# A two-layer gated mixer block on one core: another order of the first products, tile transposes and small transfers

## The reference, cut to what matters

```python
for l in range(DEPTH):                                 # DEPTH = 2
    h = rmsnorm(x, norm_mix[l])
    x = x + hybrid_mixer(h, w_in[l], ...)              # splits h @ w_in into r_i, g_v, r_f, r_q, g_q, g_k, g_a, m_i, s_u, ...
    h = rmsnorm(x, norm_xattn[l])
    x = x + cross_attention(h, rmsnorm(mem, norm_mem[l]), xattn_w_q[l], xattn_w_kv[l], xattn_w_o[l])
    h = rmsnorm(x, norm_mlp[l])
    x = x + sq_relu_mlp(h, mlp_w1[l], mlp_w2[l])
return rmsnorm(x, norm_final)
```

## Time and profile before

| | us |
|---|---|
| median of 3 runs | 1950.54 |
| the three runs | 1950.54, 2742.40, 1949.77 |
| the profiled execution, device time | 1949.91 |
| its span | 1948.10 |
| TensorE busy in it | 1931.3 (99%) |
| VectorE, ScalarE, GpSimd busy | 1249.7, 961.8, 1127.9 |

### The profile page before, as it was taken

One profiled execution on the slowest core, in us unless ns is written; L12 is line 12 of the kernel. 1 busy time (PEld: TensorE's weight loads), 2 busy tenths in 40 slices (PEclk: granted clock), 3 DMA queues, 4 the chain that ended last, 5 costly groups with the idle time before them and its releaser, 6 DMA issues.

```text
span 1948.1 us, 33275 instructions
## 1 busy us (share of the span) xinstructions
PE 1931.3 (99%) x12707; PEld 1641.5 (84%) x12707; DVE 1249.7 (64%) x1909; ACT 961.8 (49%) x1665; POOL 1127.9 (58%) x1356
## 2 busy tenths in 40 slices
PE   7999999999999999999999999999999999999998
PEld 6788788888888889999887887888898888999997
DVE  5888778856145766767358786787641556667661
ACT  6754645345445644444456647353554655344334
POOL 4565564956834555766565555467576355566653
PEclk9999999999999999999999999999999999999999
DMA  6423233333422333333342233333343233333332
GB/s 187 119 73 85 82 83 88 87 109 107 148 82 81 99 99 102 99 103 98 98 102 79 72 87 82 81 83 87 120 130 124 66 98 95 111 104 98 103 98 81
DMA packets 196091, 191.41 MB, mean 98 GB/s; under 512 B 23834, under 2 KB 186204, under 8 KB 195548
## 3 DMA queue, kind: packets, MB, share of 16 engines
q1 hardware_dynamic: 194780, 187.19, 32.7%
q10 hardware_dynamic: 1152, 2.10, 0.3%
HBM read 185.04 MB, written 3.15 MB: 97 GB/s over the span
## 4 chain that ended last, share of the span: by engine, by line
PE 95%; ACT 2%; DVE 2%; DMA 1%; issue 0%; SPq 0%; POOL 0%; DVEq 0%; ACTq 0%
PE gemm L701 73%; PE mix L701 20%; DMA w_raw<-in_w_in_dram 1%; DVE work L1974 0%; DVE work L1965 0%; PE mix L1283 0%; DMA work<-in_norm_mix_dram 0%; DVE sums_raw L1965 0%; PE mix L944 0%; PE mix L1178 0%; ACT w_hi L1429 0%; ACT work L1819 0%; DMA w_raw<-in_mlp_w_dram 0%; PE mix L877 0%; ACT work_split L1579 0%
## 5 line engine op out<-in xcount | busy, mean ns | idle before, releaser
L694 POOL TENSOR_TENSOR w_lo<-w_raw,w_hi 128x256 fp32r<-128x256 f32 x676 | 584.8, 865 | 793.0 <-ACT w_hi L1429 793.0
L695 POOL TENSOR_TENSOR w_lo<-w_raw,w_hi 128x256 fp32r<-128x256 f32 x676 | 595.8, 881 | 0.0
L701 PE MATMUL gemm<-h_hi,w_hi 128*128 128x512 f32 x1248 | 493.7, 396 | 0.5 <-DVE h_lo L1974 0.5
L701 PE MATMUL gemm<-h_lo,w_hi 128*128 128x512 f32 x1248 | 486.2, 390 | 0.0
L701 PE MATMUL gemm<-h_hi,w_lo 128*128 128x512 f32 x1248 | 486.1, 390 | 0.0
L701 PE MATMUL gemm<-work_split,w_hi 128*128 128x512 f32 (+1 forms) x1552 | 446.9, 373 | 0.3
L1429 ACT ACTIVATE w_hi<-w_raw 128x512 fp32r<-128x512 f32 x676 | 380.0, 622 | 62.8 <-DMA w_raw<-in_w_in_dram 24.6
L701 PEld LDWEIGHTS gemm<-work_split,w_hi 128*128 128x128 f32 x1552 | 281.6, 189 | 51.0 <-DVE work_split L1974 1.1
L701 PE MATMUL gemm<-work_split,w_lo 128*128 128x512 f32 (+1 forms) x776 | 288.5, 372 | 0.0
L701 PEld LDWEIGHTS gemm<-h_hi,w_hi 128*128 128x128 f32 x1248 | 234.3, 188 | 56.7 <-issue 6.6
L701 PEld LDWEIGHTS gemm<-h_hi,w_lo 128*128 128x128 f32 x1248 | 234.3, 188 | 49.5
(11 more groups left out here) (372 smaller groups left out, 2792.9 us busy)
## 6 DMA issues: line engine op xcount, KB each, us to landing
w_raw<-in_mlp_w_dram SPq DMA_DIRECT2D x256, 256.0 KB, 2.7
w_raw<-in_w_in_dram SPq DMA_DIRECT2D x208, 256.0 KB, 2.7
w_raw<-in_xattn_w_kv_dram SPq DMA_DIRECT2D x64, 256.0 KB, 3.0
w_raw<-in_w_branch_dram SPq DMA_DIRECT2D x32, 256.0 KB, 2.7
w_raw<-in_w_out_dram SPq DMA_DIRECT2D x32, 256.0 KB, 2.7
w_raw<-in_xattn_w_q_dram SPq DMA_DIRECT2D x32, 256.0 KB, 2.8
w_raw<-in_xattn_w_o_dram SPq DMA_DIRECT2D x32, 256.0 KB, 2.7
w_raw<-in_w_in_dram SPq DMA_DIRECT2D x32, 128.0 KB, 3.5
```

The source lines that it names most:

```text
L694: pool.tensor_tensor(lo[:, 0:half], raw[:, 0:half], hi[:, 0:half].bitcast(F32), ALU.subtract)
L695: pool.tensor_tensor(lo[:, half:], raw[:, half:], hi[:, half:].bitcast(F32), ALU.subtract).then_inc(split_ready, 1)
L701: return pe.matmul(o, w, a, start=start, stop=stop, skip_group_check=True)
```

## The change

It has six parts.

1. **Products on zeros.** VectorE fills one 128x512 block of the scratch array `MG` with zeros, second of its instructions. TensorE multiplies these zeros before the first tile: twice 512 and once 256 columns, and once 512 more after the tiles are turned. The results are not used.
2. **Landing order.** Tiles are turned in the order 0, 1, 3, 2, and the gain just ahead of tile 3. The gain's load moves to ScalarE's queue, behind tiles 1 and 3.
3. **First weight unit on two queues.** Its `r_i` half comes from SyncE, its `g_v` half from ScalarE. The second halves of tiles 0 and 2 come after unit 1 in place of after unit 0.
4. **High by high first.** For layer 0, kc 0 and 1 on tiles 0 and 1, `opening` issues the high by high products of both tiles as soon as the high parts are there, then low by high, then high by low, with a wait ahead of each pair.
5. **Small transfers.** `s5_log_step` of both layers (four transfers) and the two narrow column loads are issued by ScalarE, between the high parts of units 7 and 8. The parameter rows of layer 0 come five at a time after units 8 to 11, the memory tokens after unit 11, those of layer 1 two at a time after units 15 to 24, the level masks after unit 25, and `w_a2`, `s5_b`, `s5_c` after unit 26 in place of 14. VectorE gets a wait for the masks.
6. **ScalarE's order.** `norm_hi` of layer 0 writes `h_hi` before it feeds the next unit, and `first` is 4 in place of 2, so that four columns stand ahead of `values_out("r_i")`.

The core of the diff:

```diff
-            sp.wait_ge(p_vec, 1)
-            sp.dma_start(Rf(24, 1)[0:KC, 0:P], norm_mix[0].rearrange("(a b) -> a b", b=P)).then_inc(p_x[0], 16)
@@ sync, unit 0
-                        for n in range(2):
+                        for n in range(2 if u else 1):
@@ sync, places of the small transfers
-                    if u == 0:
+                    if u == 1:
                         for t in (0, 2):
                             sp.dma_start(Rf(2 * t + 1, 1), x[0, t * P:(t + 1) * P, 512:]).then_inc(p_x2, 16)
                     if u == 8:
+                        sp.wait_ge(p_pe, 1)
+                        rows0, rows1 = param_rows(0, p_rows), param_rows(1, p_x[1])
+                    if 8 <= u < 12:
+                        for _ in range(5):
+                            next(rows0, None)
+                    if u == 11:
                         sp.dma_start(R(20, 4).rearrange("p (t a) b -> p t (a b)", t=2),
                                      mem[0].rearrange("(t p) d -> p t d", p=P)).then_inc(p_rows, 16)
-                        sp.wait_ge(p_pe, 1)
-                        for _ in param_rows(0, p_rows):
-                            pass
-                        rows1 = param_rows(1, p_x[1])
                         sp.wait_ge(p_pe, 7)
-                    if 13 <= u < 22:
-                        for _ in range(3):
+                    if 15 <= u < 25:
+                        for _ in range(2):
                             next(rows1, None)
+                    if u == 25:
+                        sp.dma_start(LM[:, :, :], level_masks.rearrange("p (l c) -> p l c", c=CH)).then_inc(p_dma, 16)
-                    if unit == (14 if L == 0 else 10):
+                    if unit == (26 if L == 0 else 10):
@@ tensor
+                def opening(kc, tiles):
+                    u, banks = u0 + kc, [(G[(s0, s1)[t // 2]][t % 2][:, :], slice(t * P, t * P + P)) for t in tiles]
+                    w_hi, w_lo = WHi[:, u % RING, :], WLo[:, u % RING, :]
+                    pe.wait_ge(u_hi, kc + 1)
+                    pe.wait_ge(split_hi, u + 1)
+                    for o, tok in banks:
+                        mm(o, Uhi[:, kc, tok], w_hi, start=kc == 0, stop=False)
+                    pe.wait_ge(u_ready, kc + 1)
+                    for o, tok in banks:
+                        mm(o, Ulo[:, kc, tok], w_hi, start=False, stop=False)
+                    pe.wait_ge(split_ready, u + 1)
+                    for o, tok in banks:
+                        mm(o, Uhi[:, kc, tok], w_lo, start=False, stop=False)
+            def keep_busy(n):
+                for _ in range(n):
+                    mm(G[1][1][:, :], MG[:, 7, 0:P], MG[:, 7, :])
+            pe.wait_ge(v_chain, 1)
+            keep_busy(2)
+            mm(G[1][1][:, 0:256], MG[:, 7, 0:P], MG[:, 7, 0:256])
+            for t in (0, 1, 3):
+                pe.wait_ge(p_x[t], (32, 16, 16, 32)[t])
+                if t == 3:
+                    pe.transpose(G[0][0][:, 0:P], Rf(24, 1)[:, 0:P], ident).then_inc(p_pe, 1)
+                x_columns(t, range(4), XB)
+            pe.wait_ge(p_x[2], 16)
+            for k in range(4):
+                x_columns(2, (k,), XB).then_inc(p_pe, 1)
+            keep_busy(1)
@@ scalar
+            act.wait_ge(p_vec, 1)
+            act.dma_start(Rf(24, 1)[0:KC, 0:P], norm_mix[0].rearrange("(a b) -> a b", b=P)).then_inc(p_x[3], 16)
+            act.dma_start(WR[:, 0, BW:], w_in[0][0:P, COL["g_v"]:COL["g_v"] + BW]).then_inc(raw_in[0], 16)
@@ scalar, start of layer 0
-                first = 6 if L else 2
+                if L == 0:
+                    feed(first_unit("r_i") + 8)
+                    for l, landed in ((0, p_rows), (1, p_x[1])):
+                        for a in range(2):
+                            src = s5_log_step[l].rearrange("(t a) -> a t", a=2)[a:a + 1, :]
+                            act.dma_start(SM[64 * a:64 * a + 64, 16 + 8 * l:24 + 8 * l],
+                                          src.to_broadcast([64, 8]), allow_slow_non_contiguous=True).then_inc(landed, 16)
+                    for what, wide, to in (("m_i", 8, 0), ("g_a", RANK, 8)):
+                        src = w_in[0][:, COL[what]:COL[what] + wide].rearrange("(k p) c -> p k c", p=P)
+                        act.dma_start(NW[:, :, to:to + wide], src, allow_slow_non_contiguous=True).then_inc(nw_in, 16)
+                    feed(first_unit("r_i") + 10)
+                first = 6 if L else 4
@@ vector
             do(dve.memset(R(24, 2)[:, :, 0:P], 0.0), p_vec)
+            do(dve.memset(MG[:, 7, :], 0.0))
+                if L == 0:
+                    dve.wait_ge(p_dma, 32)
                 pick(hg, 0)
```

More of the change, by code:

```diff
@@ L538, in _ @@
                 sp.dma_start(Rf(2 * t, 1), x[0, t * P:(t + 1) * P, 0:512]).then_inc(p_x[t], 16)
-            sp.wait_ge(p_vec, 1)
-            sp.dma_start(Rf(24, 1)[0:KC, 0:P], norm_mix[0].rearrange("(a b) -> a b", b=P)).then_inc(p_x[0], 16)
             def param_rows(l, landed):
                 stage = Rf(24 + l, 1)[:, 0:P]
-                for a in range(2):
-                    src = s5_log_step[l].rearrange("(t a) -> a t", a=2)[a:a + 1, :]
-                    sp.dma_start(SM[64 * a:64 * a + 64, 16 + 8 * l:24 + 8 * l],
-                                 src.to_broadcast([64, 8]), allow_slow_non_contiguous=True).then_inc(landed, 16)
-                    yield
                 for name, src in (("norm_mix", norm_mix), ("norm_xattn", norm_xattn), ("norm_mem", norm_mem),
@@ L629, in _ @@
                                      src.rearrange("(k p) c -> p k c", p=P)).then_inc(raw_in[u % RING], 16)
-                    if u == 12 or (L < DEPTH - 1 and (name, part) == ("up1_0", 0)):
-                        nl = L if u == 12 else L + 1
+                    if L < DEPTH - 1 and (name, part) == ("up1_0", 0):
+                        nl = L + 1
                         for what, wide, to in (("m_i", 8, 0), ("g_a", RANK, 8)):
@@ L778, in token_values @@
                         pe.wait_ge(gemm_free[s0][b], used0)
-                products(0, (0, 1))
-                products(1, (0, 1))
+                for kc in range(2):
+                    if now[0]:
+                        products(kc, (0, 1))
+                    else:
+                        opening(kc, (0, 1))
                 yield
@@ L947, in params @@
             def params(l):
-                pe.wait_ge(p_x[1] if l else p_rows, 16 * 22 if l else 16 * 23)
+                pe.wait_ge(p_x[1] if l else p_rows, 16 * 22)
                 pe.transpose(M[3 - l][:, 0:P], Rf(24 + l, 1)[:, 0:P], ident).then_inc(p_pe, 1)
@@ L962, in _ @@
             XB = lambda k: (M[0], M[1], M[2], M[3], M[0], M[1], M[2], M[3])[k]
-            pe.wait_ge(p_x[0], 48)
-            pe.transpose(G[0][0][:, 0:P], Rf(24, 1)[:, 0:P], ident).then_inc(p_pe, 1)
-            for t in range(TT):
-                if t:
-                    pe.wait_ge(p_x[t], 16)
-                if t < TT - 1:
-                    x_columns(t, range(4), XB)
-                else:
-                    for k in range(4):
-                        x_columns(t, (k,), XB).then_inc(p_pe, 1)
+            def keep_busy(n):
[13 more added lines that the diff above has]
+            keep_busy(1)
             for L in range(DEPTH):
@@ L1490, in norm_hi @@
                 for k in range(k0, k1):
-                    feed(first_unit("r_i") + 8 + k)
+                    if now[0]:
+                        feed(first_unit("r_i") + 8 + k)
                     act.wait_ge(*of_layer(hx_ready, k + 1))
                     do(act.activation(Hhi[:, k, :], TH[:, k % 2, :] if now[0] else M[1 + k % 2], ACT.Copy), hi_ready)
+                    feed(first_unit("r_i") + 8 + k)
             def values_out(name):
@@ L1599, in _ @@
                     t = k - 1
-                    act.wait_ge(p_x[t], 48 if t == 0 else 16)
+                    act.wait_ge(p_x[t], (32, 16, 16, 32)[t])
                     act.wait_ge(p_x2, 16 * TT)
@@ L1618, in _ @@
                 if L == 0:
-                    act.wait_ge(p_rows, 16 * 23)
+                    act.wait_ge(p_rows, 16 * 22)
                     for t in range(2):
```

1 line of the change is left out of this document (removed).

## The result

The changed kernel takes **1963.05 us** (median of 4 runs, 1961.15 to 1963.52), where the kernel before took 1950.22 beside it. The ratio is 1.0066, with a 95% interval from 1.005 to 1.0082: 12.8 us slower. The forecast of 1947.0 was wrong, and so was its range, which ended at 1952.5. The executions that were profiled differ by as much: 1962.78 after, 1949.91 before; spans 1961.0 and 1948.1. Nearly all of the 12.9 us can be found in the first 94 us.

What follows compares the result with a forecast made beforehand. TensorE, busy 1931.3 of 1948.1 us, was taken as the bound, leaving 16.8 us idle to win. 2.65 + 0.5 + 0.3 = 3.5 us off 1949.9 gave 1946.4, plus 0.6 for the median 1947.0; range 1945.5 to 1952.5.

Steps and rivals of the forecast that it cites:

- Products on zeros, tiles and gain: Opening: sixteen transposes 0.11 us apart, not 0.21, saving 1.6 us; column 0 stands at about 7.8, not 10.7.
- Unit 0: First weight unit: some 300 KB less moved ahead of it, 0.8 us, so landed at 8.2 instead of 8.98.
- First products: TensorE through the opening's products at 13.0 instead of 15.91, 2.9 us won.
- Does it stay ahead?: From the opening to `r_f`: slack covers VectorE's and ScalarE's smaller lead, so `r_f` could start at 34.85, 2.9 us early.
- rival C: The start is won but given back at a formerly covered wait, losing up to 2.9 us: about 1949.5; chance 0.10.
- the chain to 81 us: ScalarE and VectorE work ending in a parameter column; expected some 4 us earlier, removing TensorE's 0.3 us wait.
- The copy of the `r_i` results: Ahead of `r_f`: it starts 5.8 us after `h_hi` 0, at 31.1 + I; with I at 4.0, 35.1, 2.65 us early.
- I: Time ScalarE takes to issue the six small transfers from about 24 us; taken as 4.0 us.
- How long is I?: Step setting I at 4.0 us from single SyncE issues; one stall (8.9) and two (13.8) stay in the range.
- two bounds: For I: unhindered SyncE issues, 3.4 to 4.1 us together; or stalls in a full queue, 4.88 and 2.92 us seen.
- Rival A: The queue fills under ScalarE; win is 7.5 less I; one stall gives 1952.0, two 1956.9; chance 0.25.
- The other waits: TensorE's waits inside `r_f` (0.5 us, late weight unit) and at 81 us (0.3 us, parameter column) both go.

Runs made afterwards that it cites:

- e6: The changed kernel with steps in 64-byte runs (e4), without the products on zeros: 1946.65 us.
- e11: e4 with the gain behind tile 2 on SyncE and turned first, tiles in the order 0, 1, 2, 3: 1946.60 us.
- e7: e4 with the old product order for kc 0 and 1: 1946.97 us. Its text gives ScalarE's first high part in ten executions, 7.63 to 9.07 us.
- e10: e4 with unit 0 whole on SyncE and the second halves of tiles 0 and 2 right behind it, as before: 1947.76 us.
- e4: The changed kernel with each layer's steps sent as 64-byte runs to 128 rows, sorted by a VectorE copy, still on ScalarE: 1946.46 us.
- e1: The changed kernel with the two column loads back on SyncE, the step transfers staying on ScalarE: 1953.67 us.
- e2: The changed kernel with the four step transfers back on SyncE, the column loads staying on ScalarE: 1947.21 us.
- e3: The changed kernel with all six small transfers (steps and column loads) back on SyncE: 1947.30 us.
- e5: The kernel before with only the step transfers changed to 64-byte runs, on SyncE at the old place: 1949.08 us.
- e8: The changed kernel with only layer 0's pair of steps on ScalarE ahead of the column loads, layer 1's back on SyncE: 1951.61 us.
- e12: The changed kernel with 20 unused products keeping TensorE busy ahead of the transpose that waits before `r_f`: 1960.61 us.

## Why the prediction was wrong, point by point

- **Products on zeros, tiles and gain: right, but worth little.** Transposes stood 0.11 apart from 6.23 on. The 1.6 us they save lay almost wholly beside ScalarE's work and the landing of unit 0: e6 puts the zeros at 0.2 us and e11 the order of tiles and gain at 0.1, neither clear of the spread. The sum did not count the 1.6, so it was not misled.
- **Unit 0: right.** Forecast 8.2, measured 7.95, before 8.98; the ten starts named under e7 spread over 1.4 us around it, so that one reading so near is luck in part. That the gain is in the order of the bytes was the reasoning; e10, which undoes order and split together, cannot part them.
- **First products: right.** Forecast 13.0, measured 12.77 (12.46 to 13.81 in the same executions but e7, which undoes this part).
- **Does it stay ahead?** Right with wide runs: e4 has no wait between 13 and 77 us. With the 4-byte runs a part of rival C came: in e1, e2 and e3 the wait for the parameter column at the end of the chain to 81 us is 1.0, 1.0 and 0.5 us, and not gone.
- **The copy of the `r_i` results: right in its working.** From `h_hi` 0 to `r_f`, 5.8 us forecast, 5.7 measured (43.76 to 49.47). With I put in as measured, 7.5 less 18.6 is 11.1 lost; the clock's 2.0 makes 13.1 against 12.9.
- **"How long is I?": the step that failed.** It took 4.0 from the rows of single issues, 18.6 was measured. Each of the step's two bounds was a row of this trace, but the wrong one was chosen. The reason given, that the queue was empty and the pairs were always issued at once, holds for the steps themselves (2.75 us). It says nothing of what is issued behind them, and the earlier trace rows had shown just that: the pair in 1.29 us, the next transfer but one in 4.88. The sentence "ScalarE's would hold twice as many" stood beside it and should have carried the sum. Rival A had the mechanism and was given 0.25. It was under-priced too: one stall was 8.9, two 13.8. Stalls do not count by the piece. The packet counts fit a queue with room for so many runs, in which each issue waits for room for its own: while the second load, 1024 runs, stood for 10.45 us, 1109 packets left ScalarE's queue.
- **Two costs that had no term.** The step values had landed unseen before; moved, they landed so late that TensorE waited 2.4 us (3.3 in e1). The prediction priced their issue and not their landing, although TensorE's wait ahead of `r_f` names their semaphore. In the changed kernel that wait lay inside the one for ScalarE and cost nothing more; in e1 it set `r_f`. And the clock fell in the wait, which was 2.0 us.
- **The other waits: right in the number, wrong in the reason.** Both are gone in the changed kernel (0.5 and 0.3), where TensorE was 12 us late for them. The reason given was that weight units land in time once the step transfers are on the other queue. They did not: they landed 11.1 to 17.8 us after their issue, later than the 10.6 of the earlier trace rows, and in e1 the 0.5 is gone, but the wait for the parameter column grew from 0.3 to 1.0. What takes both waits away is the wide runs (e4, e5). The masks and `w_a2` caused no wait.

The range failed because its upper end allowed one stall. Of two stalls, 1956.9 was worked out and left outside, although the step on I says that two stay in the range; even that was 6 us short.

## What to carry to other kernels

Look at how many runs a transfer has and how short they are, not at its bytes: 8 KB in 2048 runs of 4 bytes held two queues, and a full row of 64 bytes for each partition, sorted out by a small copy on VectorE, cured it. When such a transfer is moved, what pays is the first thing issued behind it, and the engine that issues it: SyncE could stand for 5 us at the price of the two short waits that e5 takes away, ScalarE could not. A short stall seen on a queue with slack is a price for the queue without slack, and should go into the sum there.

## What the runs showed of the hardware

- **A full queue stops the engine that issues.** Issues that take 0.5 us took 5.34 and 10.45 us while the DMA engines were busy at a share of 0.05 and moved 0 GB/s in the emptiest stretches, and no more than 0.31 and 70 GB/s in the fullest between 28 and 42 us. No compute instruction of ScalarE ran in that time.
- **How full, and how fast it drains.** The packets on ScalarE's queue from 23 us to the end of each issue that stood give an estimate: of 3072 runs given 711 had gone at 32.17 us in the changed kernel, of 4096 1825 at 42.65; in e8, of 3072 726 at 32.54; in e12, of 3072 973 and of 4096 1699. So it held 2100 to 2400 runs each time an issue got through. In e4, which gave it 2304 in all, none stood. Runs of 4 bytes left at 103 to 113 a us (e1, e8, and 109 in the kernel before from 35 to 41 us), runs of 32 and 64 bytes at some 580 (e2). From these two numbers I could have been estimated: some 1700 to 2000 of the 4096 runs have to go first, 16 to 19 us at 106 a us, where 18.6 was measured.
- **It holds the other queue too.** In the changed kernel and in e1 SyncE's weight units landed up to 17.8 and 18.9 us after their issue, and its issues took up to 4.57 and 4.55 us, with all the 4-byte runs on ScalarE's queue. With wide runs (e4) the units at the same place landed within 5.9 us and an issue took at most 0.39. The Trainium skill (DMA: Bandwidth & Descriptors, Issuing engines are not separate DMA queues) says that the two share the same DMA engines; the traces agree, and it is the rule that the prediction used for unit 0 and not for the landing of the weight units behind 24 us. Its Rules for kernel authors say that a last dimension that is not contiguous becomes one descriptor an element, and advise against it; the 2112 packets of e1 for 2048 values agree.
- **The clock.** After 35.1 us TensorE had one transpose, at 37.47, and then nothing; the granted clock is 0.66 in the slice from 40, then 0.50 until 53 and 0.51 in the slice to 54, where work had begun again at 49.47. Kept busy in the same wait (e12), it stayed at 1.00. At the very start the granted clock is no guide: it says 1.00 before while transposes went 0.21 apart.
- **Open.** Why the count at which an issue gets through varies from 2100 to 2400, whether it is their size or the 64 partitions of each transfer that makes the runs of 4 bytes slow, and which of the DMA engines they sat on, no run here separates. The room and the drain are read from the traces of kernels made for other questions; no run varies the number of 4-byte runs beyond one pair and two.
